# Attention's output weights placed over the convolved rows, the last slices of a vector between units 14 and 15, and the last turn inside the first projected tile

## What is computed

```python
def mlstm_out(hsum, o, hn_g, w_out):
    mu = jnp.mean(hsum, -1, keepdims=True)
    var = jnp.mean(jnp.square(hsum - mu), -1, keepdims=True)
    hn = ((hsum - mu) * lax.rsqrt(var + EPS)).reshape(B, L, H * DH) * hn_g.astype(jnp.float32)
    return (o * hn.astype(o.dtype)) @ w_out
...
x_lat = x_lat + mod_lat[2] * y_lat
h_lat = modulate(rmsnorm(x_lat, g_ffn[l]), mod_lat[3], mod_lat[4])
y = moe(h_lat.reshape(B * S, D), w_router, b_router, w1[l], w3[l], w2[l])
x_lat = x_lat + mod_lat[5] * y.reshape(B, S, D)
return rmsnorm(x_lat, g_final)
```

## Time and profile before

| | us |
|---|---|
| median of 3 runs (2679.21 to 2681.84) | 2679.22 |
| the profiled execution | 2678.67 |
| its span, first to last instruction | 2677.1 |
| TensorE busy | 2464.8 (92%) |
| DVE busy | 1886.4 (70%) |
| ACT busy | 1308.8 (49%) |
| share of TensorE in the chain that ended last | 86% |
| mean granted TensorE clock | 0.954 |

### The profile page before, as it was taken

How to read it: one execution, slowest core, us unless ns; L and a number is a source line. 1 busy time by engine, 2 the same in 40 slices (tenths; PEclk the granted TensorE clock), 3 DMA queues, 4 the chain that set the end, 5 groups by cost and what they waited for, 6 DMA issues and landing times.

```text
span 2677.1 us, 29898 instructions
## 1 busy us (share of the span) xinstructions
PE 2464.8 (92%) x10787; PEld 1754.0 (66%) x10787; DVE 1886.4 (70%) x2078; ACT 1308.8 (49%) x1244; POOL 279.0 (10%) x330
## 2 busy tenths in 40 slices
PE   6999899978999999999479999998997999999993
PEld 3555444537888888888268776554445888888883
DVE  2899946457888888888466515554247888888885
ACT  3000013117777777777242223554116777777772
POOL 0535402300000000000200001000000000000001
PEclk8999999988999999999789999999997999999997
DMA  9110347359999999997921232203428999999993
GB/s 331 32 63 32 137 186 220 142 196 380 422 384 391 387 382 392 388 388 301 350 83 63 98 114 101 71 24 131 172 98 357 422 392 390 391 384 388 382 369 118
DMA packets 150549, 672.86 MB, mean 251 GB/s; under 512 B 24858, under 2 KB 34330, under 8 KB 94034
## 3 DMA queue, kind: packets, MB, share of 16 engines
q1 hardware_dynamic: 127842, 592.73, 57.2%
q0 software_dynamic: 20208, 74.98, 7.6%
q10 hardware_dynamic: 2432, 4.26, 0.4%
HBM read 612.59 MB, written 59.33 MB: 251 GB/s over the span
## 4 chain that ended last, share of the span: by engine, by line
PE 86%; DVE 4%; DMA 4%; ACT 2%; issue 1%; POOL 1%; SPq 1%; DVEq 0%; POOLq 0%; ACTq 0%
PE ps L797 82%; PE ps L972 1%; ACT arena L1257 1%; PE ps L978 1%; DMA xs_d<-arena 1%; DMA arena<-buf_d,slots 1%; DMA arena<-in_b_conv_c_dram 1%; PE ps L885 1%; DMA arena<-in_w_out_c_dram 0%; SPq L396 0%; DMA buf_d<-arena 0%; POOL arena L676 0%; PE ps L1232 0%; DMA buf_d<-arena,slots 0%; DVE arena L1678 0%
## 5 line engine op out<-in xcount | busy, mean ns | idle before, releaser
L1784 DVE TENSOR_TENSOR wl<-wx,wh 128x2048 fp32r<-128x2048 f32 x432 | 969.3, 2288 | 46.1 <-ACT wh L1257 46.1
L1257 ACT ACTIVATE wh<-wx 128x2048 fp32r<-128x2048 f32 x432 | 819.5, 1915 | 156.7 <-PE ps L797 146.2
L797 PE MATMUL ps<-arena 128*128 128x512 f32 (+5 forms) x2424 | 804.8, 504 | 29.5 <-ACT arena L1257 11.6
L797 PE MATMUL ps<-wh,xT 128*128 128x512 f32 x2304 | 735.5, 395 | 4.9 <-DVE xT L1801 4.9
L797 PEld LDWEIGHTS ps<-arena 128*128 128x128 f32 (+1 forms) x2424 | 420.1, 190 | 388.4 <-issue 351.3
L797 PEld LDWEIGHTS ps<-wh,xT 128*128 128x128 f32 x2304 | 434.7, 189 | 105.7 <-DVE xT L1801 5.7
L797 PE MATMUL ps<-wl,xT 128*128 128x512 f32 x1152 | 455.0, 395 | 0.0
L1257 ACT ACTIVATE arena<-ps 128x512 f32<-128x512 f32 (+5 forms) x271 | 165.6, 629 | 532.3 <-PE ps L797 392.0
L797 PE MATMUL ps<-wh,gT 128*128 128x512 f32 x1152 | 377.9, 399 | 0.0
L797 PEld LDWEIGHTS ps<-wl,xT 128*128 128x128 f32 x1152 | 217.3, 189 | 47.2
L797 PEld LDWEIGHTS ps<-wh,gT 128*128 128x128 f32 x1152 | 216.8, 188 | 47.2
(11 more groups left out here) (234 smaller groups left out, 2007.0 us busy)
## 6 DMA issues: line engine op xcount, KB each, us to landing
wx<-in_w_dram SPq DMA_DIRECT2D x432, 1024.0 KB, 8.3
arena<-in_w_ada_dram SPq DMA_DIRECT2D x40, 1024.0 KB, 8.6
arena<-buf_d POOLq DMA_DIRECT2D x38, 512.0 KB, 10.1
buf_d<-arena POOLq DMA_DIRECT2D x36, 512.0 KB, 7.5
craw<-in_w_in_c_dram SPq DMA_DIRECT2D x8, 2048.0 KB, 8.1
buf_d<-arena POOLq DMA_DIRECT2D x1, 14848.0 KB, 57.8
arena<-in_w_in_ab_dram SPq DMA_DIRECT2D x8, 1024.0 KB, 12.6
arena<-in_w_out_ab_dram SPq DMA_DIRECT2D x4, 2048.0 KB, 8.4
```

The source lines that it names most:

```text
L797: return pe.matmul(bank_ap, lhsT, rhs, start=first, stop=last)
L1257: return act.activation(out_, in_, f, **kw)
L1784: v.tensor_tensor(wl[:, g], wx[:, g], whs[g % NH].bitcast(F32), ALU.subtract).then_inc(m["low"], 1)
```

## The change

- In the arena woc[1] moves from 14336 to 18512 (over xc), the stream tiles, tmp and htt of chain 3 move from 22528 on to 26704 on (also over xc), its modulation rows to 45168 (over the weighed scores), and the staging place of vector 8 to 48256.
- SP loads item 35 at u = 13, ahead of woc[0], after a wait for eE 12. It loads woc[1] and the first stream tiles after a wait for sS 16 (the last scores), and waits for pV 16 only after that, ahead of the modulation rows. The wait for the last stores comes ahead of expert groups 6 to 11 instead of behind them.
- TensorE runs slices 32 to 35 at the end of u = 14, between the values of unit 14 and the transposes of unit 15.
- The waits ahead of the projection go. Each tile waits for its own turn signal (yT_ev 13 to 16), the first tile waits for the weights in two steps (k = 0 and k = 8), turn_y(15) stands at k = 6 of the first tile, and the wait for vector 8 being out of its bank at the start of the second.
- The first tile writes PSUM banks 2 and 3, the second 0 and 1, and so on; vector 9 goes to bank 2.

```diff
@@ chain_arrays
-                return dict(xt=[at(22528 + D * i, D) for i in range(2)],
-                            mod=[None] * 3 + [at(24576 + D * i, D) for i in range(3)],
-                            tmp=at(27648, D), htt=at(28672, KD, P))
+                return dict(xt=[at(26704 + D * i, D) for i in range(2)],
+                            mod=[None] * 3 + [at(45168 + D * i, D) for i in range(3)],
+                            tmp=at(28752, D), htt=at(29776, KD, P))
...
-        woc = [at(6144, KE, 512), at(14336, KE, 512)]
+        woc = [at(6144, KE, 512), at(18512, KE, 512)]
@@ SP
                 if u == 13:
+                    sp.wait_ge(eE, 12)
+                    item_load(35)
                     sp.wait_ge(pV, 12)
...
-            sp.wait_ge(eE, 16)
-            item_load(35)
-            sp.wait_ge(pV, 16)
+            sp.wait_ge(sS, 16)
             for q in range(2):
                 sp.dma_start(woc[1][:, 8 * q:8 * q + 8, :], wov[:, 8 * q:8 * q + 8, 512:1024]).then_inc(wo_in[2 + q], 16)
...
+            sp.wait_ge(pV, 16)
             sp.wait_ge(u_st[0], stored(9, 0))
             load_mods(3)
...
+            await_stores(sp, 4)
             expert_weights(1, 0, None, range(6, PAIRS))
-            await_stores(sp, 4)
@@ TensorE, project and between
+                if n == 3:
+                    pe.wait_ge(yT_ev, 13 + t - CT)
...
+                    if n == 3 and t == CT and k % 8 == 0:
+                        for q in range(2):
+                            pe.wait_ge(wo_in[2 * q + k // 8], 32)
...
+                    if what == "y":
+                        turn_y(i)
+                    if what == "vector":
+                        pe.wait_ge(u_ev, i + 1)
@@ TensorE, loop over u and behind it
-            for n in range(32, 35):
-                mods(n)
-            turn_y(15)
-            mods(35)
+                if u == 14:
+                    for n in range(32, 36):
+                        mods(n)
 
-            pe.wait_ge(yT_ev, 16)
-            pe.wait_ge(u_ev, 9)
-            for q in range(4):
-                pe.wait_ge(wo_in[q], 32)
@@ tables
-    return (4, 6, 0, 2, 0, 2)[t] if n == 1 else 2 * (t % 2)
+    return (4, 6, 0, 2, 0, 2)[t] if n == 1 else (2, 0)[t % 2]
...
+    3: {(CT, 6): [("y", 15)], (CT + 1, 0): [("vector", 8)],
+        **{(CT + i, k): [(what, i - 1)] for i in (1, 2, 3)
+           for k, what in ((6, "turn"), (7, "route"), (8, "gather"), (12, "positions"))}}}
```

More of the change, by code:

```diff
@@ L321, in vector_ps @@
             return ps[32 * c:32 * c + 2, VBANK[w], 0:UW]
-        vstage = [at(o, UW) for o in (1024, 2048, 3072, 43120, 36976, 38000, 13312, 49520, 29696, 36976)]
+        vstage = [at(o, UW) for o in (1024, 2048, 3072, 43120, 36976, 38000, 13312, 49520, 48256, 36976)]
         A_XM, A_XC = 6144, 6144 + KE * XM
@@ L2090 @@
 LN_COLS = (slice(0, S_CTX), slice(S_CTX, S))
-VBANK = (0, 1, 2, 0, 0, 2, 0, 6, 0, 0)
+VBANK = (0, 1, 2, 0, 0, 2, 0, 6, 0, 2)
 ST_OF = [0, 1, 0, 1, None, None, 0, 1, 0, 1]
@@ L2113 @@
         (5, 12): [("positions", 4)]},
-    3: {(CT + i, k): [(what, i - 1)] for i in (1, 2, 3)
-        for k, what in ((6, "turn"), (7, "route"), (8, "gather"), (12, "positions"))}}
+    3: {(CT, 6): [("y", 15)], (CT + 1, 0): [("vector", 8)],
+        **{(CT + i, k): [(what, i - 1)] for i in (1, 2, 3)
+           for k, what in ((6, "turn"), (7, "route"), (8, "gather"), (12, "positions"))}}}
 GATE_COL = (0, 2, 1, 3)
```

## The result

The changed kernel takes 2662.18 us (median of 4 runs, 2659.64 to 2664.27) against 2680.06 for the kernel before (4 runs, 2679.21 to 2681.84): a ratio of 0.9932, 95% interval 0.9915 to 0.9949. In a second set it took 2660.55 (4 runs) against 2678.82 (7 runs), 0.9929 (0.9912 to 0.9945). The forecast was 2661.8, with a range of 2658.8 to 2666.2.

A forecast was written before the change was run, and what follows sets the result against it. TensorE, and for one stretch a late-requested load of output weights, were taken as the bound from attention to the second layer's experts. 2.1 + 14.05 + 1.9 - 0.6 = 17.4 us gave 2661.8 us, range 2658.8 to 2666.2.

The forecast's parts named there:

- Unit 15's clock: Unit 15's values in attention: twelve records take 5.2 us at full clock instead of 7.23, gain 2.1 us.
- The slices: Slices of vector 8 between units 14 and 15: 3.9 us hidden in TensorE's wait for DVE, which holds 5.1.
- The gap ahead of the projection: Between unit 15's values and the projection: slices, unit 15's turn and two waits go, gain 14.05 us.
- The first tile's clock: First projected tile: 27.5 us instead of 29.4 with no pause ahead of it, gain 1.9 us.
- The turn in the tile: Unit 15's turn, put inside the first projected tile after 24 records: no wait, loss 0.6 us.
- The modulation rows: Chain from unit 15's turn to DVE's preparation: 1.0 us late on the first tile, 1.0 to spare, costs nothing.
- The rest: Other PSUM banks, moved buffers, the wait for last stores, and everything after the first tile: no cost, moves along.
- The clock falls all the same: Rival, chance 0.13: the 2.1 us of unit 15, or as much in the first tile, are not gained; 2663.9 us.
- A late transfer: Rival, chance 0.08: late weights hold the projection or late modulation rows tile 0's turn; 2664.8 us at 3 us.
- The time is given back later: Rival, chance 0.03: the experts' start hangs on something that does not move, so the end stays at 2679.2 us.
- a slower kernel: Outcome for the whole kernel, chance 0.03: the changed kernel is slower than before.

## Why the prediction was right

**The sum.** 17.4 us were worked out, 17.7 measured in the stretch: 2.44 + 14.05 + 1.67 - 0.44. The terms are right in kind; three are off by 0.15 to 0.35 us, not all in one direction. That the profiled execution took 2661.38 where 2661.3 was worked out is partly luck, since the four executions reach from 2659.64 to 2664.27.

- *Unit 15's clock:* 2.1 forecast. Unit 15's values started at 1859.32; the first projected record follows 12 records, 5.2 us, later. Before it was 7.23. From the start of unit 14's values to the end of unit 15's it is 19.13 us before (1847.43 to 1866.56) and 16.69 now (1859.32 + 5.2 - 1847.83): 2.44. The 0.4 more is the turn of unit 14, which at full clock lets the values start 0.49 us after it and not 0.91 (1858.42 to 1859.33). The prediction had left it at the low clock.
- *The slices:* hidden, as worked out. Their room was forecast at 5.1 us. They take 4.0 (1853.20 to 1857.20), and with 3.45 more unit 15's values start 3.1 later, so it is 4.0 + 3.45 - 3.1 = 4.35. Of the 0.75 that is missing, 0.4 is the turn of unit 14, which lets the values start earlier, and 0.2 are unit 14's values, which stand 5.4 us ahead of the slices and not 5.2.
- *The gap ahead of the projection:* 14.05, gone entirely. It had two walls, the load and the norm of unit 15 with its turn; taking one away leaves the other (66.65 and 64.55 us for the two kernels that keep the turn ahead, 66.92 for the one with the late load).
- *The first tile's clock:* 1.9 forecast, 1.67 measured. From its first record to DVE the tile takes 28.18 us with the turn in it (1864.52 to 1892.70), before 29.41 without it: 29.41 - 28.18 + 0.44 = 1.67. The forecast took 29.4 up to DVE's start and set it against 64 x 0.43 = 27.5, which ends with TensorE's last record; the 0.3 us between the two went into the gain by mistake.
- *The turn in the tile:* 0.6 forecast, 0.44 measured (1874.79 to 1875.23).
- *The modulation rows:* this size was off. The chain from the turn of unit 15 to DVE's preparation was forecast to end 1.0 us behind the first tile's end; it ended 4.3 us ahead (1888.4 against 1892.7), with the normed rows 1.9 us early for the turn of tile 0, so some 6 us were to spare and not 1.0. Each of its three pieces was shorter: from the turn to the store 1.5 us for 2.1, from the store to SP's load 2.9 for 5.8, from the load to the end of the first preparation 9.2 for 10.9. The sum didn't suffer, since the chain has a price only when it is late. From the start of ACT's store (1876.33) to SP's next load (1879.19) it was 2.9 us:

```profile
1876.33 1.33 ACTq L1276 DMA_DIRECT2D mods_d<-arena  x2
```

The prediction took over 5.8 from a trace in which 4 MB of weights were under way. Over the fourteen traces it is 5.8 us in the two where they were (the kernel before and the one with the slices alone) and 2.9 to 3.2 in the twelve where they had landed. The Trainium skill's figure (DMA: Bandwidth & Descriptors, Anatomy of one DMA: about 2.0 us fixed, a fit of transfers issued from GpSimd, while this one is issued from ACT) was nearer to the 2.9 than the row of before.
- *The rest:* nothing, as forecast. From DVE's start on the last tile to the first product of the experts it is 34.15 us before (1999.58 to 2033.73) and 34.12 now (1982.28 to 2016.40).

**The rivals.** *The clock falls all the same* did not come: 1.00 in all windows from 1853 to 1870. With that, the Trainium skill's account of a clock that swings when matmuls have short pauses between groups (TensorE: Matmul & The Clock Gate, A second HAM failure mode) did not describe this stretch: the wait of 0.75 us left the clock alone, and behind the wait of 2.02 us in the kernel before unit 15's turn ran at full speed too (0.66 us for its four records, where 1.11 is the low clock). Waits of 4.1 and 5.15 us did bring it down, in each run in which they stood. *A late transfer* did not hold anything, but the load landed up to 1.9 us later than in the row I took, and the run with the late turn shows that the second deadline is real. *The time is given back later* and *a slower kernel* had nothing in the trace for them: TensorE worked from 1859.32 to the end of the fourth tile without a fall of the clock.

## What to carry to other kernels

A wait that a chain of waits puts down to one DMA may hide another of nearly the same length behind it; work out what would be waited for next, and take away both, or half of the gain stays behind. Work that can stand anywhere should be put into the wait just ahead of dense products: there it costs nothing as far as it fits (4.35 us here), and here it kept the clock up for what follows, while a wait of four or five us was paid for once in its length and a second time in 1.5 to 2.6 us of low clock. Where the start of a program shifts by several us between executions, compare a stretch from one fixed instruction to another, not single times.

## What was unexpected of the hardware

- Filling is not a sure way to keep the clock. Two kernels that differ by one product had the same wait of 2.45 us ahead of the experts' first products; in one the clock was 1.00 behind it and in the other 0.57 over 4 us, 56.61 against 57.50 us for the stretch. What decides isn't settled here.
- The same load of 2 x 2 MB landed after 7.7 to 7.9 us (first half) and 12.7 to 13.4 (second) in four kernels, and after 8.5 to 10.0 and 13.4 to 14.9 in the ten others. In the ten SP had issued the last load of gates 0.4 us ahead of it, in the four at least 3.5 us ahead. No run changes that alone, so the cause isn't shown.
